# Two blocks of a hybrid network: setup reordered, the norms' weight splits moved, and idle products added

## The reference, cut to what matters

```python
def first_block(x, ...):                       # layers (0, 0) and (0, 1)
    for layer in range(2):
        h = rms_norm(x, norm_g[layer])
        proj = h @ w_in[layer]                 # 1024 x 8704
        ... attention, short convolution, retention, gates, w_branch ...
        x = x + merged @ w_out[layer]
    return rms_norm(x, final_norm_g)

def second_block(x, positions, ...):           # layers (1, 0) and (1, 1)
    cos, sin = rope_tables(positions)
    for l in range(2):
        x = x + 0.5 * swiglu(rmsnorm(x, ffn1_norm[l]), ffn1_w_gu[l], ffn1_w_down[l])
        x = x + hybrid_mixer(rmsnorm(x, mix_norm[l]), cos, sin, w_in[l], ...)
        x = x + 0.5 * swiglu(rmsnorm(x, ffn2_norm[l]), ffn2_w_gu[l], ffn2_w_down[l])
    return rmsnorm(x, final_norm)
```

## Time and profile before

| what | us |
|---|---|
| median of 3 runs (range) | 2120.64 (2118.78 to 2124.33) |
| the profiled execution, its own time | 2121.72 |
| its span in the profile | 2119.9 |
| TensorE busy in the span | 2037.2 (96%) |
| VectorE busy | 1183.1 (56%) |
| ScalarE busy | 869.6 (41%) |
| GpSimd busy | 201.0 (9%) |
| mean granted TensorE clock | 0.987 of full |

### The profile page before, as it was taken

How to read it: one execution, slowest core, us unless ns; L and a number is a source line. 1 busy time by engine, 2 the same in 40 slices (tenths; PEclk the granted TensorE clock), 3 DMA queues, 4 the chain that set the end, 5 groups by cost and what they waited for, 6 DMA issues and landing times.

```text
span 2119.9 us, 38391 instructions
## 1 busy us (share of the span) xinstructions
PE 2037.2 (96%) x16700; PEld 1895.3 (89%) x16700; DVE 1183.1 (56%) x1541; ACT 869.6 (41%) x1264; POOL 201.0 (9%) x218
## 2 busy tenths in 40 slices
PE   4999999999989999899999999999999999999998
PEld 4999989999879998799988999899988999888997
DVE  4476355674365557754536655555568545356555
ACT  3544224443144345553423443443446443324443
POOL 0300013000100002400101000000013111110000
PEclk9999999999999999999999999999999999999999
DMA  4545445444446554333323566465544333235663
GB/s 158 176 161 175 158 145 179 159 161 164 154 150 190 187 180 155 109 121 100 106 86 130 178 187 190 144 191 183 184 155 143 101 101 101 101 120 159 180 194 133
DMA packets 347582, 320.53 MB, mean 151 GB/s; under 512 B 9899, under 2 KB 317592, under 8 KB 347416
## 3 DMA queue, kind: packets, MB, share of 16 engines
q1 hardware_dynamic: 345640, 317.60, 47.0%
q10 hardware_dynamic: 1776, 0.48, 0.1%
HBM read 317.01 MB, written 1.05 MB: 150 GB/s over the span
## 4 chain that ended last, share of the span: by engine, by line
PE 93%; DVE 2%; ACT 1%; issue 1%; DMA 1%; POOL 1%; ACTq 0%; SPq 0%; DVEq 0%; POOLq 0%
PE banks L1087 24%; PE banks L1088 24%; PE banks L1089 24%; PE banks L1082 10%; PE banks L1537 3%; PE banks L1108 3%; DVE ring_low L1968 1%; PE banks L1265 1%; PE banks L1252 1%; POOL stat_all L2517 1%; ACT ring_high L1665 1%; DMA pos_i<-in_positions 1%; PE banks L1603 0%; PE banks L1261 0%; PE banks L1141 0%
## 5 line engine op out<-in xcount | busy, mean ns | idle before, releaser
L1968 DVE TENSOR_TENSOR ring_low<-ring,ring_high 128x2048 fp32r<-128x2048 f32 x272 | 628.0, 2310 | 380.8 <-ACT ring_high L1665 379.2
L1087 PE MATMUL banks<-h_high,ring_high 128*128 128x256 f32 x2720 | 780.3, 287 | 0.0
L1088 PE MATMUL banks<-hT_low,ring_high 128*128 128x256 f32 x2720 | 769.7, 283 | 0.0
L1089 PE MATMUL banks<-h_high,ring_low 128*128 128x256 f32 x2720 | 769.5, 283 | 0.0
L1665 ACT ACTIVATE ring_high<-ring 128x2048 fp32r<-128x2048 f32 x272 | 519.0, 1908 | 212.8 <-PE banks L1089 137.5
L1087 PEld LDWEIGHTS banks<-h_high,ring_high 128*128 128x128 f32 x2720 | 521.6, 192 | 6.4 <-issue 2.6
L1088 PEld LDWEIGHTS banks<-hT_low,ring_high 128*128 128x128 f32 x2720 | 521.5, 192 | 1.8 <-issue 0.5
L1089 PEld LDWEIGHTS banks<-h_high,ring_low 128*128 128x128 f32 x2720 | 521.0, 192 | 0.0
L1665 ACT ACTIVATE scratch<-banks 128x256 f32<-128x256 f32 (+3 forms) x302 | 129.9, 449 | 313.3 <-PE banks L1108 125.9
L1087 PE MATMUL banks<-ring_high,h_high 128*128 128x256 f32 (+1 forms) x768 | 241.5, 314 | 2.3 <-DVE hT_low L1968 2.3
L1088 PE MATMUL banks<-ring_low,h_high 128*128 128x256 f32 (+1 forms) x768 | 235.5, 307 | 0.0
(11 more groups left out here) (191 smaller groups left out, 1852.4 us busy)
## 6 DMA issues: line engine op xcount, KB each, us to landing
ring<-in_w_in SPq DMA_DIRECT2D x122, 1024.0 KB, 5.0
ring<-in_ffn_w_gu SPq DMA_DIRECT2D x176, 512.0 KB, 4.8
ring<-in_ffn_w_down SPq DMA_DIRECT2D x44, 1024.0 KB, 4.8
ring<-in_w_out SPq DMA_DIRECT2D x16, 1024.0 KB, 4.8
ring<-in_w_branch SPq DMA_DIRECT2D x12, 1024.0 KB, 4.9
ring<-in_w_br_mla SPq DMA_DIRECT2D x4, 1024.0 KB, 5.2
ring<-in_w_br_fox SPq DMA_DIRECT2D x4, 1024.0 KB, 5.0
ring<-in_w_br_dn SPq DMA_DIRECT2D x4, 1024.0 KB, 4.8
```

What stands on the lines that cost most here:

```text
L1087: pe.matmul(acc, lhs[0], rhs[0], start=start, stop=False)
L1088: pe.matmul(acc, lhs[0], rhs[1], start=False, stop=False)
L1089: return pe.matmul(acc, lhs[1], rhs[0], start=False, stop=stop)
L1968: return dve.tensor_tensor(o, i0, i1, op)
```

## The change

1. **Norms with half steps.** `sl` of the second piece stands ahead of `sq 3`, the first `dh` and the variance; the variance `rs 1` stands ahead of `xt 1 0`.
2. **Norms without.** `sh` of the second piece stands behind `xm 1`. A new step `kb` has TensorE make products whose result is overwritten: 7 ahead of `rn 1`, 11 behind it, of 256 columns each, into the bank of `gu f 0`.
3. **Setup.** The order of layer (0, 0)'s norm is written out as `FIRST`. SP's queue begins with the constants that are needed at once (`ident`, `minus_half`), x in two halves and the eight rows of the first gain; two weight pieces follow, then the other tables and rows, then pieces 2 and 3. TensorE first turns only the eight gain rows. All other setup work becomes steps `set 0` to `set 4` behind `d` 1, 3, 4, 5 and 6.

```diff
     if half_steps:
-        out += [("nl", m, 0, 0), ("nl", m, 0, 1), ("sh", second), q(3, 1), ("sq", m, 3), half_steps[0], ("xt", m, 1, 0),
-                ("rs", m, 1), ("sl", second), ("xt", m, 1, 1), ("rn", m, 1), half_steps[1],
+        out += [("nl", m, 0, 0), ("nl", m, 0, 1), ("sh", second), q(3, 1), ("sl", second), ("sq", m, 3), half_steps[0],
+                ("rs", m, 1), ("xt", m, 1, 0), ("xt", m, 1, 1), ("rn", m, 1), half_steps[1],
                 ("xm", m, 1, 0), ("xm", m, 1, 1), ("nl", m, 1, 0), ("nl", m, 1, 1)]
     else:
-        out += [("xt", m, 1, 0), q(3, 1)] + xe(3) + [("sq", m, 3), ("sh", second), ("nl", m, 0, 0), ("rs", m, 1),
-                ("xt", m, 1, 1), ("nl", m, 0, 1), ("rn", m, 1), ("xm", m, 1, 0), ("xm", m, 1, 1), ("nl", m, 1, 0),
-                ("nl", m, 1, 1), ("sl", second)]
+        out += [("xt", m, 1, 0), q(3, 1)] + xe(3) + [("sq", m, 3), ("nl", m, 0, 0), ("rs", m, 1),
+                ("xt", m, 1, 1), ("nl", m, 0, 1), ("kb", m, 0), ("rn", m, 1), ("kb", m, 1), ("xm", m, 1, 0), ("xm", m, 1, 1), ("sh", second),
+                ("nl", m, 1, 0), ("nl", m, 1, 1), ("sl", second)]
...
+FIRST = [("sq", 0, 0), ("sq", 0, 1), ("xt", 0, 0, 0), ("xt", 0, 0, 1), ("rs", 0, 0), ("sq", 0, 2), ("xt", 0, 1, 0),
+         ("sq", 0, 3), ("rs", 0, 1), ("xt", 0, 1, 1), ("rn", 0, 0), ("sh", ("in", 0)), ("xm", 0, 0, 0), ("xm", 0, 0, 1),
+         ("nl", 0, 0, 0), ("nl", 0, 0, 1), ("rn", 0, 1), ("sl", ("in", 0)), ("dh", 0), ("sh", ("in", 1)),
+         ("xm", 0, 1, 0), ("xm", 0, 1, 1), ("sl", ("in", 1)), ("nl", 0, 1, 0), ("nl", 0, 1, 1), ("dh", 1)]
+SETUP_AFTER = {("d", 1): 0, ("d", 3): 1, ("d", 4): 2, ("d", 5): 3, ("d", 6): 4}
...
+            EARLY = CONST_AT["causal"][0]
+            sp.dma_start(const[:, 0:EARLY], a["consts"][:, 0:EARLY]).then_inc(setup_const.sem, 16)
+            for t in range(TT):
+                sp.dma_start(xv[:, t], a["x"][0, t * P:(t + 1) * P]).then_inc(setup_x[t].sem, 16)
...
+            load_rows(0, 0, "norm_g", 8, setup_gain)
...
                 for n, piece in enumerate(PLANS[L[0]].pieces[:RING]):
...
+                    if n == 2 and before is None:
+                        load_tables()
...
+            def keep_busy(L, m, i):
+                first = ("gu", m // 2, 0)
+                if i == 0:
+                    arrived(L, first)
+                    claim(L, first)
+                w = weights_split(L, first, KD, 256)[0]
+                for _ in range((7, 11)[i]):
+                    pe.matmul(bank_of(L, first)[:, 0:256], w[:, 0, 0:P], w[:, 1], start=True, stop=True)
...
                 arrived(L, ("in", o))
+                if (L, o) == ((0, 0), 3):
+                    pe.wait_ge(setup_par.sem, 2)
...
+            def parameters_turned(L, i):
+                if i == 0:
+                    pe.wait_ge(setup_dma.sem, ROWS_LANDED)
+                    pe.wait_ge(setup_par.sem, 1)
+                    for i, n in enumerate((NR1, NR1, NR2, NR2)):
+                        mm = pe.transpose(bank[3][:, i * P:i * P + n], par_rows[0:n, i, :], ident[0:n, 0:n])
+                    mm.then_inc(setup_pe.sem, 1)
...
+            pe.wait_ge(setup_const.sem, 16)
+            pe.wait_ge(setup_gain.sem, 16)
+            pe.transpose(bank[3][:, 0:8], par_rows[0:8, 0, :], ident[0:8, 0:8]).then_inc(setup_pe.sem, 1)
...
             def d1(L, o):
                 if o == 3:
+                    pool.wait_ge(setup_tables.sem, 32)
```

More of the change, by code:

```diff
@@ L457, in program @@
         steps = boundary(last, 0, *((ffn_leads(0),) if L[0] else LEADS1), scaled=L == (1, 0))
-        out += [(LAYERS[n - 1], s) if s[0] in ("wl", "dl") else (L, s) for s in steps if n or s[0] != "wl"]
+        out += [(LAYERS[n - 1], s) if s[0] in ("wl", "dl") else (L, s) for s in (steps if n else FIRST)]
         start = PLANS[L[0]].entry + 1
-        out += [(L, s) for s in order[start:len(order) - 8]]
+        for s in order[start:len(order) - 8]:
+            out.append((L, s))
+            if n == 0 and s in SETUP_AFTER:
+                out.append((L, ("set", SETUP_AFTER[s])))
         last = ("dl", 1) if L[0] else ("wl",)
@@ L487, in shape_constants @@
     add("ident", np.eye(P))
+    add("minus_half", np.full((P, 16), -0.5))
     add("causal", np.concatenate([np.zeros((P, P)), np.where(j > i, NEG, 0.0)], 1))
@@ L929, in build @@
         setup_dma = Signal("setup_dma")
-        setup_x = Signal("setup_x")
+        setup_x = [Signal(f"setup_x{t}") for t in range(TT)]
+        setup_gain = Signal("setup_gain")
+        setup_tables = Signal("setup_tables")
+        setup_par = Signal("setup_par")
         setup_pe = Signal("setup_pe")
@@ L2468, in _, with angles @@
+            def angles(i):
+                two_pi = 2.0 * math.pi
+                c1 = float(np.float32(6.28125))
+                c2 = float(np.float32(np.floor((two_pi - c1) * 2 ** 21) / 2 ** 21))
+                c3 = float(np.float32(two_pi - c1 - c2))
+                magic = 12582912.0
+                k_, t_ = turns[:, i], trig[:, i]
+                setup_link(dve.tensor_scalar(k_, ang[:, :, :], 1.0 / two_pi, (0.25, 0.0)[i], ALU.mult, ALU.add))
                 setup_link(dve.tensor_scalar(k_, k_, magic, None, ALU.add))
@@ L2501, in _, with factors @@
-            g_ = par2[:, :, PAR2["b_gate_2"]:PAR2["b_gate_2"] + 24]
-            setup_link(dve.tensor_scalar(g_, g_, 0.5, None, ALU.mult))
+                if i:
+                    ins.then_inc(setup_dve.sem, 1)
+                else:
+                    setup_link(ins)
+            def factors():
+                dve.wait_ge(setup_act.sem, 1)
+                for l in range(DEPTH):
+                    dst = par1[:, l, PAR1["neg_lam"]:PAR1["neg_lam"] + 1]
+                    setup_link(tt(dst, le[:, l, 1:2], le[:, l, 0:1], ALU.subtract))
+                    setup_link(dve.tensor_scalar(dst, dst, -LAMBDA_INIT[l], None, ALU.add))
+                    g_ = par1[:, l, PAR1["subln"]:PAR1["subln"] + A_V]
+                    dve.tensor_scalar(g_, g_, 1.0 - LAMBDA_INIT[l], None, ALU.mult)
+                    g_ = par2[:, l, PAR2["neg_a"]:PAR2["neg_a"] + 8]
+                    dve.tensor_scalar(g_, g_, -1.0, None, ALU.mult)
+                    g_ = par2[:, l, PAR2["o_norm"]:PAR2["o_norm"] + HD]
+                    dve.tensor_scalar(g_, g_, 0.5, None, ALU.mult)
+                dve.wait_ge(setup_act.sem, 2)
+                for half_ in range(2):
+                    dve.tensor_copy(pcos[:, :, n_f * half_:n_f * (half_ + 1)], trig[:, 0])
+                dve.tensor_copy(psin[:, :, :], trig[:, 1])
+                setup_link(dve.tensor_scalar(pnsin[:, :, :], trig[:, 1], -1.0, None, ALU.mult))
@@ L2503, in _ @@
+            parts1["set"] = set_up
+            dve.wait_ge(setup_pe.sem, 1)
+            setup_link(dve.tensor_copy(par1[:, 0, 0:8], bank[3][:, 0:8]))
+            dve.sem_inc(setup_par.sem, 1)
             for L, step in program("DVE"):
```

122 lines of the change are left out of this document (53 added, 69 removed).

## The result

The changed kernel takes 2085.7 us (median of 4 runs, 2083.35 to 2087.34), where the kernel before, run beside it, takes 2121.76 (4 runs, 2118.78 to 2124.33). The ratio is 0.983, 95% interval 0.9813 to 0.9847: 1.7% faster. The forecast was 2086.0 with a range of 2077 to 2098. The profiled execution took 2086.32; its span is 2084.5, mean granted clock 0.992.

A forecast was written before the change was run, and what follows sets the result against it. TensorE, holding 93% of the chain, was taken as the bound, with time won only where its products stop or run slowly. Savings of 16.6 + 7.0 + 1.8 + 10.2 = 35.6 us from 2121.72 gave 2086, range 2077 to 2098.

The forecast's parts named there:

- Setup: Start of the kernel: first two weight pieces' products end at 34.3 instead of 50.95, saving 16.6 us; bounds 13.3 to 20.
- rival C: Congested start: piece 0 lands at 16, 3.5 us later, or small rows delay piece 2, 3 us more; 2093; 12%.
- the middle row of 174 GB/s: Setup: queue rate seen at 6 to 8 us, taken for piece 0, which would land at 12.5.
- The row of 19 GB/s: Setup: queue rate seen between 8 and 12 us; if nothing large flows until 12, piece 0 lands at 15 or 16.
- Rival A: Setup: nothing large was held back, piece 0 lands at 9.0 and the setup gains 20 us; 2082.5; 13%.
- no change at all: Whole kernel time unchanged: would need 63 us, or piece 0 landing at 42; 1%.
- Half-piece norms: Three norms: low part ahead of the variance shortens GpSimd's root and TensorE's pause, 2.35 us each, 7.0 us in all.
- `sh` behind x: Feed-forward norms: x's high part no longer waits behind the weights' high part where weights are late; 1.8 us, once.
- `kb`: Feed-forward norms: 7 and 11 idle products take 0.84 and 1.32 us inside pauses of 1.07 and 1.53, costing nothing.
- The clock: Half clock behind six of seven norms goes: 4.2 us behind half-piece norms, 6.0 of 7.0 behind the others; 10.2 us.
- Rival B: Feed-forward norms: the clock falls despite the idle products, the 6.0 us are lost; 2092 to 2097; 15%.
- Falls elsewhere: Middle of the run: four clock falls may come or go as work shifts, 1.5 us each, counted as zero.

The follow-up runs named there:

- experiment 9: Changed kernel with ScalarE's seven small broadcasts issued behind the second dense piece, in `set 0`, instead of at the start; 2082.73 us.
- experiment 10: Changed kernel with ScalarE's seven small broadcasts issued behind x's last high parts of the setup instead of at the start; 2078.12 us.
- experiment 3: Changed kernel with the old order in the norms with half pieces, the second piece's low part behind the variance again; 2099.34 us.
- experiment 4: Changed kernel with the second piece's low part behind the root and both products by the gain in the half-piece norms; 2096.51 us.
- experiment 5: Changed kernel with the weights' high part ahead of x's again in the feed-forward norms, idle products kept; 2087.38 us.
- experiment 8: Changed kernel with the idle products doubled, 14 and 22 instead of 7 and 11; 2087.74 us.
- experiment 1: Changed kernel with both orders of the norms as before and no idle products, only the new setup kept; 2107.63 us.
- experiment 2: Changed kernel with both `kb` steps, the idle products, taken out; 2096.17 us.
- experiment 6: Changed kernel with only the 7 idle products ahead of the root's spread, none behind it; 2087.34 us.
- experiment 7: Changed kernel with only the 11 idle products behind the root's spread, none ahead of it; 2087.51 us.
- experiment 11: Experiment 10's kernel with the first block's last gain loaded ahead of the weights of layer (1, 0) on SP's queue; 2076.93 us.

## Why the prediction was right, by its steps

*The sum.* The 35.6 us forecast meets the 35.4 of the span closer than its terms do. The setup gave 1.7 less than forecast, the clock 1.0 more and the half-piece norms 0.25 more. That these cancel is luck. That the steps themselves came out as described is not, but for the start of the setup.

*Setup: 16.6 forecast, 14.9 measured.* Two errors of opposite sign. First, piece 0 landed at 16.0 and not at 12.5: + 3.5 us. That is the upper bound that the prediction gave, and the condition of rival C, but the mis-sized term stands ahead of it. x and the gains precede piece 0 on SP's queue. They were forecast at 6.3, from the 264 GB/s of the constants in the trace of before; the core moved 122 GB/s from 2 to 4 us and 228 from 4 to 6, and x's second half landed at 9.2, 2.9 us late. From there to piece 0's landing it took 6.8 us where 6.2 was forecast, so the middle row of 174 GB/s was nearly right. The row of 19 GB/s was no large transfer held back: in the trace of before, what SP's queue moved between 8 and 12 us is 26 KB in packets of 512 bytes and less, its own small rows, and x's packets start at 13.1. Rival A read that row rightly, and still its outcome did not come. Experiments 9 and 10 show the cause: with the broadcasts out of the way x is there at 6.2 and piece 0 at 10.2 and 9.7, near rival A's 9.0. Second, the chain behind the landing took 6.0 us and not 7.6. The kernel's description puts VectorE's product by the root into `rn`; the rows show it in `xm`. In `FIRST` the one for the second half therefore stands behind the low part of piece 0 (21.89, behind 19.69), not ahead of it, and the 1.3 us counted for it were not on the path. From the first product to the start of the third piece, with the parameters' four transposes between, it took 14.0 where 14.2 was forecast. In sum 3.5 - 1.6 - 0.2 = 1.7 less gain. The moved setup work and the tables cost nothing, as said: piece 2's high part was made at 24.95, and TensorE did not stop at `d` 2. The two parts of rival C were thus met by half: piece 0 late, piece 2 in time. One working of the prediction does not come out: for no change at all piece 0 would have to land at 12.5 + 35.6 = 48, not at 42; only a chance of 1% rests on it.

*Half-piece norms: 7.0 forecast, 7.25 measured.* The root took 0.56 and the pause 0.76, as written (0.56 and 0.8). Experiments 3 and 4 show the mechanism from both sides.

*`sh` behind x: 1.8 forecast, 1.8 measured*, once (experiment 5: a pause of 1.82; the 1.7 between the medians are within their spread). Its cover held: the second piece's split never stopped TensorE there.

*`kb`: nothing forecast, nothing measured.* The norms take 3.34 us as before. Experiment 8 shows the edge: 18 products more cost 1.0 to 1.3 us a norm.

*The clock: 10.2 forecast, 11.2 measured.* The 4.2 behind the half-piece norms came. Of the 7.0 behind the others I counted 6.0, and all came. Rival B did not occur. That the idle products, and not the position in time, hold the clock is shown by experiments 1 and 2, and by the mean clock of all their runs. Their worth was read from the falls of before; in experiment 2, on the new schedule, it was 10.5.

*Falls elsewhere: zero forecast, 0.2 measured.*

*Open.* Which pauses bring a fall. Experiments 6 and 7 rule out that the last pause alone decides, since falls came with it filled and stayed away twice with it open. They rule out too that less idle time in all is enough, since experiment 7 left less of it than experiment 6 and had more falls. Each group alone was too little. Yet one pause of 1.82 brought none (experiment 5), and in experiment 11 a fall stood in a norm with all its idle products. With one profile of each kernel, and falls that differ from one trace to the next, this can't be settled here.

## What to carry to other kernels

Look at what the cheap instructions wait beside: one GpSimd operation on one column set a pause of TensorE, and moving two steps of VectorE's stream cut it from 3.17 us to 0.76 three times. A stop of TensorE costs its own length and, where half clock follows it (behind most norms with pauses over 1 us here), 1.5 to 3 us more, so overwritten products in a pause that can't be removed may pay more than the pause itself did. In a start-up, ask of every small transfer whether it is needed before the first large one, and then place the late ones with a wait in mind: late enough to be out of the way, early enough that nothing waits for them.

## What the runs showed of the hardware

**Small broadcasts slow a large transfer on another queue.** With seven broadcasts of 1 to 256 KB in flight on ScalarE's queue the core moved 165 to 217 GB/s from 6 to 12 us and piece 0 (1 MB) landed at 16.0; without them 311 to 408 GB/s and 9.7 (the changed kernel and experiment 10). SP's issuing was slower too: its transfer of the constants took 6.79 us to issue, 3.34 without them. The Trainium skill (DMA: Bandwidth & Descriptors, Queues, rings and completion order) says that each DMA engine takes turns between the queues by packets. No run here shows the turns themselves. They do not explain the loss: between 6 and 12 us the mean busy share of the DMA engines was 0.58 to 0.66 in the changed kernel and 0.97 to 1.11 in experiment 10. So the engines were not filled up by small packets; they stood idle for about a third of the time. What kept work from them, the slower issuing or something behind it, stays open.

**A one-column GpSimd operation waits for VectorE's two-input subtraction in SBUF.** It took 2.54 us beside the low part (128x2048, both inputs from `ring` and `ring_high`) and 0.56 beside the product by the gain, which reads a bank (experiments 3 and 4). The Trainium skill (SBUF — State Buffer, SBUF: two separate sides) says that VectorE with two inputs from there and a reading GpSimd hold a shared pair of ports in turn, each for its whole instruction. The traces agree: the root ends 0.4 us behind the subtraction.

**The clock after short pauses.** With a pause of 1.07 us or more (1.40 in the first norm), two products and a pause of at least 1.53, half clock came in 12 of 12 norms of three kernels (before, experiments 1 and 2); it began 0.2 to 3.2 us behind the start of the two products. With pauses of 0.22 to 0.25 (0.56 ahead of the spread in each kernel's first norm, 1.82 once in experiment 5) it came in 1 of 28 norms of seven kernels (the changed one and experiments 3, 4, 5, 9, 10 and 11).
